# 64 unused bytes ahead of the split weights of a two-layer hybrid decoder trunk

## The chip, the cores and the metric

The kernel runs on one core of one Trainium2 chip. The metric is the device time of one execution in microseconds (us); lower is better. The timed runs of the kernel before agree within 0.3 us, so a difference of 0.2%, some 2.4 us, can be told from none.

## The reference, cut to what matters

512 tokens of width 1024 go through two layers. Each layer is a token mixer (mLSTM in the first, differential attention in the second) beside a cross-attention into 256 memory tokens, an output projection and a SwiGLU feed-forward of hidden width 2816:

```python
for i in range(DEPTH):                       # two layers
    h = rmsnorm(x, norm1[i])
    mix, xq = mlstm_mixer(h, ...) if i % 2 == 0 else diff_attention(h, positions, ...)
    xo = memory_cross_attention(xq, mem, ...)
    x = x + jnp.concatenate([mix, xo], axis=-1) @ w_out[i]
    h = rmsnorm(x, norm2[i])
    gu = h @ w_gate_up[i]
    x = x + (jax.nn.silu(gu[..., :FFN_HIDDEN]) * gu[..., FFN_HIDDEN:]) @ w_down[i]
```

All is float32. Nearly all arithmetic is in the products of activations with weights.

## The kernel before

**Split operands.** A float32 operand is kept as the sum of two rounded ones, a high and a low part, both in the type F32R. A product of two such operands is three matmuls that accumulate in the same PSUM bank: weights high by tokens high, weights high by tokens low, weights low by tokens high. For each matmul TensorE first loads its 128 x 128 stationary operand (the weights) and then streams the moving operand (the tokens) past it. The profile lists the two as PEld LDWEIGHTS and PE MATMUL, and writes the moving operand first: `PS<-Hh,w_hi` streams Hh past w_hi.

**Three kinds of product use the split weights.**

- *Dense products*, by `tile` (L1948), with 512 moving columns. The tokens are Hh and Hl (the normalised input, 560 sets of three) or Ah and Al (mixer output or hidden units, 480 sets of three). They make the projections, the output projections, the first gate and up tiles of each feed-forward, and all down tiles.
- *Memory products*, by `m_tile` (L1983), through the same `tile`, with 256 moving columns out of Ah and Al: 64 sets of three.
- *Block products*, by `pair` (L2262, matmul at L2284), with 256 moving columns. For 16 of 22 hidden chunks of each layer, the gate and up tiles are made together in a Strassen-like scheme: seven block products with tokens tc_hi and tc_lo and weights w_hi and w_lo, each of four steps k of three matmuls. That is 2 layers x 16 x 7 x 4 = 896 sets of three.

The matmuls of the first two kinds are recorded under the helper's line L1946, with the attention's matmuls, which use no split weights; the block products have L2284 to themselves. Beside them, in the first 17 us, `wg` (the eight gate columns, padded to 128) is multiplied with Hh and Hl, 16 matmuls.

**Where operands lie.** SBUF tensors are taken one after the other in the order of the code (L276 to L283 and on), each rounded up to 32 bytes a partition, so a tensor's byte address in its partition follows from the sizes ahead of it. Of the operands of the F32R products:

| tensor | address before | modulo 256 | step from one operand to the next |
|---|---|---|---|
| Hh, Hl, Ah, Al | 17,536; 33,920; 50,304; 66,688 | 128 | 2048 B dense, 1024 B memory |
| w_raw (weights as loaded) | 83,072 | 128 | 512 B |
| w_hi, w_lo | 99,456; 113,792 | 128 | 512 B |
| tc_hi, tc_lo | 169,152; 197,824 | 192 | 1024 B |
| wg | 218,112 | 0 | 512 B |

All steps are multiples of 256 bytes, so every operand of a tensor has the tensor's place modulo 256. Dense and memory products have weights at 128 and tokens at 128; block products have weights at 128 and tokens at 192; the gate columns have weights at 0 and tokens at 128.

**Order of the work.** Each engine's program is written out by hand. SyncE loads weight tiles from HBM into the four slots of w_raw. GpSimd (POOL) splits them for dense tiles (L778 writes w_hi, L783 writes w_lo) and forms sums and differences of weight tiles for the block products (L736 to L743) and part of their low parts (L748); ScalarE and VectorE round and split the rest and move PSUM to SBUF. Semaphores carry the order.

```python
w_raw = sb("w_raw", [P, RAW, 8, P])
wq_hi = sb("w_hi", [P, 28, P], F32R)
wq_lo = sb("w_lo", [P, 28, P], F32R)
```

Of the kernel before, what the change touches and what calls it, by code (L numbers as in the profile page):

```python
# [32 lines left out]
P = 128  # L33
# [230 lines left out]
def hybrid_trunk(nc, x_t, mem_t, positions, wt, wg_cols, a_gate_b, b_lambda, prm_cols, con, out):  # L264
    ctx = ExitStack()
    with ctx:
        def sb(name, shape, dt=F32, scope=ctx):
            return scope.enter_context(nc.sbuf_tensor(name, shape, dt))
# [10 lines left out]
        Ah = sb("Ah", [P, 8, SEQ], F32R)  # L279
        Al = sb("Al", [P, 8, SEQ], F32R)  # L280
        w_raw = sb("w_raw", [P, RAW, 8, P])
        wq_hi = sb("w_hi", [P, 28, P], F32R)
        wq_lo = sb("w_lo", [P, 28, P], F32R)  # L283
        w_hi = wq_hi[:, 0:8 * SPLIT].rearrange("p (s k) m -> p s k m", k=8)
# [2331 lines left out]
```

## Time and profile before

| | us |
|---|---|
| median of 3 runs (1202.67 to 1202.94) | 1202.91 |
| the profiled execution, as timed | 1204.02 |
| its span, first to last instruction | 1202.2 |
| TensorE matmul (PE) busy | 1196.8 |
| GpSimd (POOL) busy | 857.4 |
| VectorE (DVE) busy | 755.9 |
| ScalarE (ACT) busy | 502.4 |

A matmul's own duration in these tables, say 389 ns, runs from its start to its last result, and matmuls overlap in the array. What one costs in a stream is the distance between the starts of neighbours; it is read from the timeline, or from a piece of the chain of waits divided by its count.

### The profile page before, as it was taken

The page shows a single profiled execution, that of the slowest core. Times are in us where ns is not written, and L with a number is a line of the kernel's source. Part 1 is how long each engine was busy: PE and PEld are TensorE (multiplying, and loading weights), DVE is VectorE, ACT ScalarE, POOL GpSimd, SP SyncE. Part 2 cuts the span into 40 slices and gives each one's busy share as a digit, 9 for nine tenths or more (in the row PEclk, how much of TensorE's full clock was granted, in tenths as well). Part 3 has the DMA queues.
Part 4 walks back from the last instruction along what each step waited for, and adds up shares of the span by engine and source line. Part 5 has one row for each costly group of instructions (what it writes and reads, how often), then busy time and mean ns, then how long its engine had stood idle before and what let it go on. Part 6 is the DMA issues. An engine that isn't in the chain of part 4 may idle for free.

```text
span 1202.2 us, 18736 instructions
## 1 busy us (share of the span) xinstructions
PE 1196.8 (100%) x6998; PEld 1032.9 (86%) x6998; DVE 755.9 (63%) x1099; ACT 502.4 (42%) x1012; POOL 857.4 (71%) x873
## 2 busy tenths in 40 slices
PE   9999999999999999999999999999999999999998
PEld 7888887788889998899888777778888899889997
DVE  7954434645737991599335888874674599348931
ACT  7522456733203551355231666644431255125510
POOL 7998433566878996699676444445688799669965
PEclk9999999999999999999999999999999999999999
DMA  7234211132223333233433222232232333322332
GB/s 282 92 123 157 71 36 53 53 106 79 92 83 106 106 106 123 88 106 106 126 103 97 80 71 71 64 80 69 71 100 79 118 106 107 105 89 98 115 105 85
DMA packets 35097, 117.43 MB, mean 98 GB/s; under 512 B 4417, under 2 KB 4930, under 8 KB 34886
## 3 DMA queue, kind: packets, MB, share of 16 engines
q1 hardware_dynamic: 33416, 112.83, 29.2%
q10 hardware_dynamic: 1598, 3.51, 1.2%
q8 instruction: 51, 0.84, 0.3%
q14 instruction: 32, 0.26, 0.1%
HBM read 111.07 MB, written 2.11 MB: 94 GB/s over the span
## 4 chain that ended last, share of the span: by engine, by line
PE 97%; DVE 1%; ACT 1%; issue 0%; ACTq 0%; POOL 0%; POOLq 0%
PE PS L1946 69%; PE PS L2284 26%; PE PS L2385 1%; DVE Al L1564 0%; PE PS L2194 0%; PE PS L2413 0%; PE PS L2354 0%; DVE nmB L1850 0%; PE PS L2019 0%; PE PS L2346 0%; PE PS L2338 0%; DVE PB L1862 0%; ACT tmp L1010 0%; ACT tmp L1018 0%; DVE PB L1861 0%
## 5 line engine op out<-in xcount | busy, mean ns | idle before, releaser
L783 POOL TENSOR_TENSOR w_lo<-w_raw,w_hi 128x256 fp32r<-128x256 f32 (+1 forms) x516 | 394.7, 796 | 11.0
L778 POOL TENSOR_SCALAR w_hi<-w_raw 128x1024 fp32r<-128x1024 f32 (+2 forms) x132 | 142.1, 1076 | 283.4 <-PE PS L1946 275.0
L2284 PE MATMUL PS<-tc_hi,w_hi 128*128 128x256 f32 x896 | 250.9, 280 | 0.0
L2284 PE MATMUL PS<-tc_hi,w_lo 128*128 128x256 f32 x896 | 250.0, 279 | 0.0
L2284 PE MATMUL PS<-tc_lo,w_hi 128*128 128x256 f32 x896 | 250.0, 279 | 0.0
L1946 PE MATMUL PS<-Hh,w_hi 128*128 128x512 f32 x560 | 229.3, 410 | 0.0
L1946 PE MATMUL PS<-Hl,w_hi 128*128 128x512 f32 x560 | 219.1, 391 | 0.0
L1946 PE MATMUL PS<-Hh,w_lo 128*128 128x512 f32 x560 | 219.0, 391 | 0.0
L1946 PE MATMUL PS<-Ah,w_hi 128*128 128x512 f32 (+1 forms) x544 | 208.0, 382 | 0.1
L1946 PE MATMUL PS<-Ah,w_lo 128*128 128x512 f32 (+1 forms) x544 | 205.0, 377 | 0.0
L1946 PE MATMUL PS<-Al,w_hi 128*128 128x512 f32 (+1 forms) x544 | 204.9, 377 | 0.0
L2284 PEld LDWEIGHTS PS<-tc_hi,w_lo 128*128 128x128 f32 x896 | 168.5, 188 | 0.0
L2284 PEld LDWEIGHTS PS<-tc_hi,w_hi 128*128 128x128 f32 x896 | 168.2, 188 | 0.2
L2284 PEld LDWEIGHTS PS<-tc_lo,w_hi 128*128 128x128 f32 x896 | 167.6, 187 | 0.2
L1619 DVE TENSOR_TENSOR xT<-xT,PS 128x512 f32<-128x512 f32 x64 | 43.9, 687 | 159.4 <-PE PS L1946 159.4
L1946 PEld LDWEIGHTS PS<-Hh,w_hi 128*128 128x128 f32 x560 | 105.6, 189 | 27.6 <-issue 7.8
L1946 PEld LDWEIGHTS PS<-Hh,w_lo 128*128 128x128 f32 x560 | 105.4, 188 | 22.8
L1946 PEld LDWEIGHTS PS<-Hl,w_hi 128*128 128x128 f32 x560 | 105.7, 189 | 20.2 <-issue 1.0
L748 POOL TENSOR_TENSOR w_lo<-tmp,w_hi 128x512 fp32r<-128x512 f32 x64 | 107.7, 1700 | 17.9 <-ACT w_hi L1099 17.9
L1946 PEld LDWEIGHTS PS<-Ah,w_hi 128*128 128x128 f32 x544 | 102.3, 188 | 20.7 <-issue 1.5
L1946 PEld LDWEIGHTS PS<-Ah,w_lo 128*128 128x128 f32 x544 | 102.3, 188 | 19.0
L1946 PEld LDWEIGHTS PS<-Al,w_hi 128*128 128x128 f32 x544 | 102.4, 188 | 18.6 <-issue 0.5
(300 smaller groups left out, 1805.5 us busy)
## 6 DMA issues: line engine op xcount, KB each, us to landing
w_raw<-in_wt_dram SPq DMA_DIRECT2D x181, 512.0 KB, 3.6
w_raw<-in_wt_dram SPq DMA_DIRECT2D x16, 384.0 KB, 3.0
w_raw<-in_wt_dram SPq DMA_DIRECT2D x8, 448.0 KB, 3.3
QKR<-QKP ACTq DMA_DIRECT2D x24, 128.0 KB, 4.8
xT<-in_x_t_dram SPq DMA_DIRECT2D x8, 256.0 KB, 4.8
out_dram<-xT SPq DMA_DIRECT2D x8, 256.0 KB, 2.0
mT<-in_mem_t_dram SPq DMA_DIRECT2D x1, 1024.0 KB, 9.5
cn<-in_constants_dram SPq DMA_DIRECT2D x1, 594.5 KB, 6.9
```

The source lines that it names most:

```text
L748: nc.gpsimd.tensor_tensor(wq_lo[:, b:b + 4], pair_source(n, q), wq_hi[:, b:b + 4].bitcast(F32), ALU.subtract).then_inc(s_low_p, 1)
L778: nc.gpsimd.tensor_scalar(w_hi[:, sl, 0:nk], w_raw[:, raw, 0:nk], 0.0, 1.0, ALU.add, ALU.mult).then_inc(w_round, 1)
L783: lo = nc.gpsimd.tensor_tensor(w_lo[:, sl, w], w_raw[:, raw, w], w_hi[:, sl, w].bitcast(F32), ALU.subtract)
L1619: nc.vector.tensor_tensor(xT[:, k], xT[:, k], PS[:, bank], ALU.add).then_inc(dense_free, 1)
L1946: return nc.tensor.matmul(out_, a, b, start=start, stop=stop)
L2284: last = nc.tensor.matmul(out_, w[:, b + k], a[:, q, k], start=q < 4 and k == 0 and j == 0, stop=k == 3 and j == 2, skip_group_check=q > 3)
L2385: last = nc.tensor.transpose(PS[:, 2 + u % 2, k * P:(k + 1) * P], PB[:, 0, W_OFF[u] + k * P:W_OFF[u] + (k + 1) * P], ident)
```

## The change

One tensor of 16 float32 a partition, 64 bytes, is put between w_raw and w_hi. Nothing reads or writes it.

```diff
@@ -279,6 +279,7 @@
         Ah = sb("Ah", [P, 8, SEQ], F32R)
         Al = sb("Al", [P, 8, SEQ], F32R)
         w_raw = sb("w_raw", [P, RAW, 8, P])
+        sb("shift_w", [P, 16])
         wq_hi = sb("w_hi", [P, 28, P], F32R)
         wq_lo = sb("w_lo", [P, 28, P], F32R)
         w_hi = wq_hi[:, 0:8 * SPLIT].rearrange("p (s k) m -> p s k m", k=8)
```

xT, Hh, Hl, Ah, Al and w_raw stay where they are; every tensor behind moves up by 64 bytes. The built programs have the same 10,478 instructions in the same order on every engine, with the same waits; only addresses differ, and line numbers by one.

| product | weights, tokens modulo 256 before | after | tokens minus weights before | after |
|---|---|---|---|---|
| dense, memory | 128, 128 | 192, 128 | 0 | -64 |
| block | 128, 192 | 192, 0 | +64 | +64 |
| gate columns | 0, 128 | 64, 128 | 128 | +64 |

## Rows read from the trace of the kernel before

**Rows 1.** The page's part 1: engine, busy us, share of the span, instructions.
```profile
PE 1196.8 (100%) x6998; PEld 1032.9 (86%) x6998; DVE 755.9 (63%) x1099; ACT 502.4 (42%) x1012; POOL 857.4 (71%) x873
```

**Rows 2.** Waits of TensorE, whole span: waited for, us in total, times, longest.
```profile
PE PS L1946 <- POOL hpi L700: 1.0, 1, 1.0
PE PS L1946 <- ACT PB L1216: 0.5, 1, 0.5
PE PS L2385 <- ACT ATB L1225: 0.4, 1, 0.4
```

**Rows 3.** The chain of waits: start us, us, what, instructions in the piece.
```profile
377.26 79.15 PE PS L2284 x672
499.97 79.15 PE PS L2284 x672
...
953.63 79.15 PE PS L2284 x672
1076.34 79.15 PE PS L2284 x672
```

**Rows 4.** Groups of TensorE matmuls by form: shapes, count | busy us, mean ns | idle.
```profile
L2284 PE MATMUL PS<-tc_hi,w_hi 128*128 128x256 f32 x896 | 250.9, 280 | 0.0
...
L1946 PE MATMUL PS<-Hh,w_hi 128*128 128x512 f32 x560 | 229.3, 410 | 0.0
...
L1946 PE MATMUL PS<-Ah,w_hi 128*128 128x512 f32 x480 | 188.7, 393 | 0.1
...
L1946 PE MATMUL PS<-Ah,w_hi 128*128 128x256 f32 x64 | 19.3, 302 | 0.0
```

**Rows 5.** Timeline, memory products (start us, us, instruction); ten like them left out.
```profile
52.54 0.28 PE L1946 MATMUL PS<-Ah,w_lo 128*128 128x256 f32 x1
52.66 0.28 PE L1946 MATMUL PS<-Ah,w_hi 128*128 128x256 f32 x1
...
53.98 0.28 PE L1946 MATMUL PS<-Ah,w_lo 128*128 128x256 f32 x1
```

**Rows 6.** Timeline, dense products of a down stage; 47 left out.
```profile
469.66 0.39 PE L1946 MATMUL PS<-Ah,w_lo 128*128 128x512 f32 x1
...
480.54 0.39 PE L1946 MATMUL PS<-Ah,w_lo 128*128 128x512 f32 x1
```

**Rows 7.** Timeline, last block product and first dense ones behind it.
```profile
1032.50 0.28 PE L2284 MATMUL PS<-tc_hi,w_lo 128*128 128x256 f32 x1
1032.62 0.40 PE L1946 MATMUL PS<-Ah,w_hi 128*128 128x512 f32 x1
1032.86 0.39 PE L1946 MATMUL PS<-Al,w_hi 128*128 128x512 f32 x1
...
1034.24 0.39 PE L1946 MATMUL PS<-Al,w_hi 128*128 128x512 f32 x1
1034.47 0.39 PE L1946 MATMUL PS<-Ah,w_lo 128*128 128x512 f32 x1
```

**Rows 8.** Timeline of the start: dense products and gate columns in turn; nine left out.
```profile
11.94 0.39 PE L1946 MATMUL PS<-Hh,wg 128*128 128x512 f32 x1
...
14.27 0.39 PE L1946 MATMUL PS<-Hh,wg 128*128 128x512 f32 x1
```

**Rows 9.** Stretches: length, busy (x) of PE, PEld, DVE, ACT, POOL, PEclk, DMA, GB/s.
```profile
14.00:16.00 2.00, 2.00 (x10) 1.60 (x9) 1.90 (x4) 0.96 (x2) 2.00 (x3) 1.00 1.06 446
...
19.00:20.00 1.00, 1.00 (x6) 0.84 (x5) 0.65 (x1) 0.00 (x0) 1.00 (x2) 1.00 1.02 406
```

**Rows 10.** The same view: first block stage, a down stage, the second layer's attention.
```profile
377.00:456.00 79.00, 79.00 (x672) 78.96 (x671) 67.91 (x92) 41.47 (x82) 74.15 (x51) 1.00 0.32 113
456.00:500.00 44.00, 44.00 (x198) 36.49 (x197) 13.19 (x16) 7.20 (x11) 26.30 (x30) 1.00 0.27 87
...
650.00:830.00 180.00, 178.91 (x1043) 140.24 (x1042) 138.76 (x255) 105.73 (x279) 84.37 (x100) 0.99 0.26 71
```

**Rows 11.** Timeline, attention scores: tokens and stationary operand both at 192, two half-height matmuls each.
```profile
663.17 0.28 PE L1946 MATMUL PS<-QR_LO,QT_HI 64*128 64x256 f32 x2
663.29 0.28 PE L1946 MATMUL PS<-QT_HI,QR_LO 64*128 64x256 f32 x2
```

**Rows 12.** Timeline, the first products after the gate columns; three left out.
```profile
18.45 0.39 PE L1946 MATMUL PS<-Hh,w_lo 128*128 128x512 f32 x1
...
19.36 0.39 PE L1946 MATMUL PS<-Hh,w_hi 128*128 128x512 f32 x1
```

**Rows 13.** The page's part 5, the split of the low parts on GpSimd.
```profile
L783 POOL TENSOR_TENSOR w_lo<-w_raw,w_hi 128x256 fp32r<-128x256 f32 (+1 forms) x516 | 394.7, 796 | 11.0
```

## The prediction, on record before the result

> **What bounds the kernel now.** I read the page's busy shares first: TensorE's matmuls are busy 1196.8 of 1202.2 us, the next engine 857.4 [rows 1]. Then TensorE's waits: 1.9 us in all, in three waits [rows 2]. The chain of waits says the same from the other end, with whole stages in single pieces of TensorE, 672 block products in 79.15 us four times over [rows 3]. So the time is the number of matmuls times what each costs in the stream. No other engine matters until TensorE becomes quicker than it. The granted clock is 1.00 in all stretches used here, the 2.4 GHz level [rows 9, 10].
>
> **What one matmul costs, and what of it is not columns.** Durations in the groups [rows 4] overlap and don't serve; distances of starts do.
>
> - Memory products, 256 columns: twelve steps from 52.54 to 53.98 us, 1.44 / 12 = 120.0 ns each [rows 5].
> - Dense products, 512 columns: 48 steps from 469.66 to 480.54 us, 10.88 / 48 = 226.7 ns each [rows 6].
> - Their difference, 106.7 ns for 256 columns, is 0.417 ns a column, one period of 2.4 GHz. So 256 columns are 106.7 ns, 512 are 213.3 ns, and either kind pays the same 13.3 ns on top.
> - Block products, 256 columns as well: 79.15 us / 672 = 117.8 ns [rows 3], only 11.1 ns on top.
>
> Memory and block products have the same shape, the same kinds of operand and a weight load each. What differs is where the tokens lie: 128 modulo 256 for the first, 192 for the second, with weights at 128 in both. Over a set of three the block products save 3 x 2.22 = 6.7 ns, which is the time of 16 columns, and 16 columns of tokens are 64 bytes. That such a round figure comes out is my reason to take the surplus for something that hangs on addresses in steps of 64 bytes, and not for a property of the stage.
>
> **Place or distance?** The surplus could hang on where the tokens lie, where the weights lie, or how far they are apart. The attention scores have tokens and stationary operand both at 192, and one pair follows the other after 0.12 us at 256 columns [rows 11]: 120 ns, as where both are at 128. These are half-height matmuls, two side by side, so it is a weak witness, but it speaks for distance: 0 gives 13.3, +64 gives 11.1. The third distance is seen at the start. There two of five products use the gate columns, with weights at 0 and tokens at 128, distance 128, and ten steps take 14.27 - 11.94 = 2.33 us, 233.0 ns each, 19.7 ns on top [rows 8]. DMA isn't the reason: its engines are full then and are still full at 19 to 20 us [rows 9], when the gate columns are over and four steps from 18.45 to 19.36 us take 0.91 us, 227 ns each [rows 12]. So distances of 0, +64 and 128 are seen, and the dense products go to the one that is not seen, -64.
>
> **The change, part by part.**
>
> 1. *Dense and memory products, distance 0 to -64.* They are 3120 and 192, 3312 in all (each count in the table of groups is one of three) [rows 4]. The nearest rows are 11.1 ns (distance +64) and 19.7 ns (a mix with 128) against 13.3 now. If -64 is as good as +64, that is -2.22 x 3312 = -7.4 us. If it is as bad as the mix with 128, it is (233.0 - 226.7) x 3312 = +20.9 us. I take -7.4 us: one step of 64 bytes off alignment is what the better row has, to one side, and the other side is equally one step off.
> 2. *Block products, +64 kept, but tokens from 192 to 0 and weights from 128 to 192.* By distance this costs nothing. Bounds: losing the whole surplus, 2688 x 11.1 = -29.8 us; going to the memory products' 120.0 ns, +5.9 us. I take 0, by the row in which both operands at 192 cost what both at 128 cost [rows 11].
> 3. *Gate columns, distance 128 to +64.* Sixteen matmuls among 24 dense ones; if all forty come from 233.0 to 224.4 ns, -0.3 us. Left out.
> 4. *Products whose two operands both move* (attention scores, transposes, sums over partitions) keep their distance: 0.
> 5. *Splits on GpSimd, rounding on ScalarE and VectorE.* They write w_hi and w_lo at 192 instead of 128 and read w_raw where it was. I have no row of one operation at both places, so from below and above a few per cent either way. The cover is TensorE: in a block stage GpSimd is busy 74.15 of 79.0 us, in a down stage 26.3 of 44 [rows 10]. A split slower by up to 6% stays hidden; beyond that each block stage would end with GpSimd. 0.
> 6. *DMAs.* They fill w_raw, which stays; the few between moved tensors stand behind waits that cost 1.9 us in all [rows 2]. 0.
> 7. *Transients.* After a stage ends, the dense products don't take 226.7 ns at once: behind a block stage seven steps from 1032.62 to 1034.24 us take 231.4 each [rows 7]. In the second layer's attention, dense products stand between short matmuls and are mostly in that state (1043 matmuls in 180 us) [rows 10]. What the shift makes of them isn't seen; I price them like the steady ones.
>
> Sum: -7.4 us against the execution that was profiled (span 1202.2, timed at 1204.02). That one is 1.1 us above the median, and a saving per matmul carries over unchanged: 1202.9 - 7.4 = 1195.5 us.
>
> One rule speaks against any effect. TensorE has two SBUF read ports, one for the moving operand and one for weights, and loading the next weights takes nothing from the running matmul (the Trainium skill, TensorE: Matmul & The Clock Gate, step-by-step: what each phase is for). By it the sum would be 0 and the time 1202.9 us. The trace doesn't agree so far as it goes: two streams of one shape cost 120.0 and 117.8 ns.
>
> **The rivals.**
>
> *Nothing moves, 1202.9 us.* The 2.2 ns would then be the block stage's own, from the tensors' distance in whole kilobytes or the way banks are taken in turn, or -64 would cost what 0 costs. For it: one pair of kinds is thin evidence. Against it: the gate columns differ from dense products in address and in bank alone, and they cost more [rows 8, 12].
>
> *The wrong side: dense products slower, 1210 to 1224 us.* With tokens 64 bytes behind the weights instead of ahead, the two reads could meet where now they pass. Seen around the circle of 256 bytes, the surplus is 13.3 at 0, 11.1 at +64 and high at 128; -64 lies between 0 and the high one, with no low neighbour but 0. One step of 16 columns more on each of 1104 sets is +7.4 us, 1210.3. Staying at the 233.0 ns of the start is +20.9, 1223.8; if the attention stages, already near that, lose nothing, about half is left, 1213. It decides from the point at which the dense distance goes above 227 ns; GpSimd can't offset it. This is nearly as likely as my forecast.
>
> *Place counts in the block products.* Tokens at 0 begin a stretch of 256 bytes. If half the surplus goes, 2688 x 5.5 = -14.9 us, but GpSimd's 74.15 of 79.0 us caps the gain at 4.9 us a stage, 19 us in all [rows 10]: with dense unchanged about 1188. If they go to 120.0 ns, 1208.8. For: nothing; against: rows 11.
>
> **How the numbers follow.** Forecast (dense and memory gain one step, block unchanged) 0.33, with its own range 1193 to 1199; no change 0.18; dense slower 0.32, a third of that near 1210 and the rest up to 1224; block products faster, alone or with the dense, 0.11; block products slower 0.06. Faster by over 0.2% is 0.33 + 0.11 = 0.44, slower 0.32 + 0.06 = 0.38, within 0.2% (all that a measurement can tell from no change) 0.18. Cases of both signs hold most of the chance. The range is 1189 to 1221: it leaves out the far end of the slow case, about 0.1, and large gains in the block products or in the dense beyond one step, about 0.08.
>
> **What would show it.** In the changed kernel's timeline a steady stretch of dense products should show 224.4 ns from start to start instead of 226.7, memory products 117.8 instead of 120.0, and the four block pieces of the chain 79.15 us again. TensorE's waits should stay near 2 us. Dense at 226.7 means no effect; at 229 or 233 the wrong side. Block pieces away from 79.15 us mean that the place counts, and then the sum above is built on the wrong variable. GpSimd's mean for a low part well away from its 796 ns [rows 13] would say that its writes depend on the place too.

## The result, and the profile after

| | before | changed |
|---|---|---|
| median, us | 1202.84 (1202.67 to 1202.94, 4 runs) | 1218.01 (1217.85 to 1219.42, 4 runs) |
| span of the profiled execution, us | 1202.2 | 1216.1 |

The changed kernel takes 1.0127 times as long, 95% interval 1.0113 to 1.0141: 15.2 us slower. The forecast was 1195.5 us, faster.

The page's busy shares and TensorE's waits of the changed kernel, as in [rows 1, 2]:

```profile
PE 1210.7 (100%) x6998; PEld 1030.9 (85%) x6998; DVE 754.8 (62%) x1099; ACT 502.1 (41%) x1012; POOL 857.2 (70%) x873
...
PE PS L1947 <- POOL hpi L701: 1.0, 1, 1.0
PE PS L1947 <- ACT PB L1217: 0.5, 1, 0.5
PE PS L2386 <- ACT ATB L1226: 0.4, 1, 0.4
```

TensorE is 13.9 us busier, every other engine is as busy as before to 2 us, and the waits are the same three to a tenth. Nothing became late; the matmuls themselves take longer. The chain of waits (start us, us, what, instructions) says which. The rows of after:

```profile
383.29 79.14 PE PS L2285 x672
462.44 44.80 PE PS L1947 x192
507.23 79.15 PE PS L2285 x672
...
1044.24 44.80 PE PS L1947 x192
1089.04 79.14 PE PS L2285 x672
```

and the down stage between the same block stages before, which is not among the rows above:

```profile
456.41 43.56 PE PS L1946 x192
```

Three of the four block stages are what they were in [rows 3], 79.15 us; the third is not one piece here and comes further down. The down stage, 192 dense products, went from 43.56 to 44.80 us, 1.24 us. The timeline gives the price of one product (start us, us, instruction; 44 rows left out), in the changed kernel:

```profile
475.34 0.40 PE L1947 MATMUL PS<-Ah,w_lo 128*128 128x512 f32 x1
...
485.84 0.39 PE L1947 MATMUL PS<-Ah,w_lo 128*128 128x512 f32 x1
```

45 steps in 10.50 us are 233.3 ns each, where [rows 6] had 226.7: 20.0 ns over the columns' 213.3 instead of 13.3. The 256-column memory products went the other way. Twelve steps of the changed kernel:

```profile
87.08 0.28 PE L1947 MATMUL PS<-Ah,w_hi 128*128 128x256 f32 x1
...
88.44 0.28 PE L1947 MATMUL PS<-Ah,w_hi 128*128 128x256 f32 x1
```

1.36 / 12 = 113.3 ns, where [rows 5] had 120.0. That is this stretch; in others of the changed kernel many memory products still take 118 ns.

**Which profile to compare with.** The medians are 15.2 us apart, the two profiled spans only 13.9. The profiled execution of the kernel before lost time to something else. Its windows (length, busy and count of PE, PEclk, DMA, GB/s):

```profile
780.00:792.00 12.00, 11.58 (x72) 1.00 0.51 121
...
793.00:796.00 3.00, 3.00 (x12) 0.50 0.41 108
```

For some 3.4 us the granted clock is 0.50, the 1.2 GHz level, and before it TensorE had been busy in 80.00 of the 80 us from 700 to 780. This is the 0.99 that [rows 10] show for 650 to 830 us. The changed kernel's profile has no such stretch, so a comparison by stage needs another one. Run e13 below has all addresses modulo 256 as before, a median of 1203.1 us, a granted clock of 1.00 in 780 to 800 us and a span of 1200.8 us. Its chain, and then that of the changed kernel at the third block stage:

```profile
377.56 79.15 PE PS L2285 x672
...
579.41 75.96 PE PS L1947 x349
...
952.24 79.15 PE PS L2285 x672
```

```profile
965.43 13.62 PE PS L2285 x120
```

By stage, from starts of the pieces: the first 377.6 us (1248 dense and all 192 memory products) grew by 5.7 us, the three down stages between and behind block stages by 1.2 each, the stretch from the second to the third block stage (1296 dense products) from 372.8 to 379.1 us, by 6.2, and the third block stage shrank by 0.3. The sum is 15.3 us, which is the spans' difference, 1216.1 - 1200.8.

3120 dense products at +6.7 ns would be 20.8 us. Averages over all starts in the two traces say what is missing. Outside the down stages, 2307 dense products are followed at once by another dense one; this step went from 227.6 to 233.3 ns, which is 13.2 us, and the down stages add 3.7. The other 237 are followed by a product of another kind or by a longer step, and those hardly changed. The step of 227.6 instead of 226.7 ns comes from the attention stages: in the second layer's, 650 to 830 us, 319 such steps averaged 229.8 ns, while in the stretches on either side it was 226.8. The memory products gave 0.8 us back.

GpSimd's split of low parts took what it took in [rows 13]:

```profile
L784 POOL TENSOR_TENSOR w_lo<-w_raw,w_hi 128x256 fp32r<-128x256 f32 (+1 forms) x516 | 394.9, 796 | 11.0
```

### The profile page after: what moved, and what is told of

It reads as the page before. It is cut to its first block, busy times and chain, and to the rows that moved or that the text cites. A ratio compares the mean times of both kernels' runs of the same rounds, so it can differ in the third digit from the quotient of the medians.

```text
span 1216.1 us, 18736 instructions
## 1 busy us (share of the span) xinstructions
PE 1210.7 (100%) x6998; PEld 1030.9 (85%) x6998; DVE 754.8 (62%) x1099; ACT 502.1 (41%) x1012; POOL 857.2 (70%) x873
## 4 chain that ended last, share of the span: by engine, by line
PE 98%; DVE 1%; DMA 0%; issue 0%; ACT 0%; POOL 0%; ACTq 0%; SPq 0%; DVEq 0%; POOLq 0%
PE PS L1947 70%; PE PS L2285 26%; PE PS L2386 1%; PE PS L2195 0%; PE PS L2414 0%; DMA w_raw<-in_wt_dram 0%; DVE nmB L1851 0%; PE PS L2355 0%; PE PS L2347 0%; PE PS L2020 0%; PE PS L2339 0%; DVE PB L1863 0%; PE PS L2158 0%; PE PS L2155 0%; DVE PB L1862 0%
## 5 line engine op out<-in xcount | busy, mean ns | idle before, releaser
L1947 PE MATMUL PS<-Al,w_hi 128*128 128x512 f32 (+1 forms) x544 | 207.5, 381 | 0.0
L1947 PE MATMUL PS<-Ah,w_lo 128*128 128x512 f32 (+1 forms) x544 | 207.5, 381 | 0.0
```

The costliest lines, as they stand in the source:

```text
L1947: return nc.tensor.matmul(out_, a, b, start=start, stop=stop)
```

## The experiments

All differ from the kernel before by unused bytes alone, with the same instructions in the same order. The diffs that show a `-` line start from the changed kernel, the others from the kernel before. `[P, n]` is n float32, 4n bytes. "Distance" is tokens minus weights modulo 256. The columns "192 dense" and "672 block" are pieces of the chain of waits, a down stage and a block stage.

| run | weights | dense distance | block distance | 192 dense, us | 672 block, us | median, us | ratio, 95% |
|---|---|---|---|---|---|---|---|
| before | 128 | 0 | +64 | 43.56 | 79.15 | 1202.9 | |
| changed | 192 | -64 | +64 | 44.80 | 79.14 | 1218.0 | 1.0127 (1.0113 to 1.0141) |
| e1_w192 | 64 | +64 | +64 | 43.96 | 77.86 to 78.85 | 1207.2 | 1.0037 (1.0023 to 1.0051) |
| e2_w128 | 0 | 128 | +64 | 44.62 | 79.15 | 1216.4 | 1.0113 (1.0092 to 1.0133) |
| e3_w_only | 192 | -64 | 0 | 44.80 | 80.63 | 1224.1 | 1.0176 (1.0159 to 1.0193) |
| e4_all64 | 192 | 0 | +64 | 43.56 | 79.15 | 1202.7 | 0.9997 (0.9987 to 1.0006) |
| e5_tc64 | 128 | 0 | -64 | 43.52 | 79.15 | 1202.5 | 0.9997 (0.9987 to 1.0006) |
| e6_tc0 | 128 | 0 | 128 | 43.56 | 80.64 | 1209.0 | 1.0051 (1.0031 to 1.0071) |
| e7_dense_m32 | 160 | -32 | +32 | 44.80 | 78.40 | 1215.8 | 1.0107 (1.0087 to 1.0128) |
| e9_tc160 | 128 | 0 | +32 | 43.55 | 78.40 | 1199.9 | 0.9975 (0.9966 to 0.9985) |
| e10_tc96 | 128 | 0 | -32 | 43.57 | 79.52 | 1204.9 | 1.0016 (1.0007 to 1.0026) |
| e11_tc224 | 128 | 0 | +96 | 43.56 | 80.64 | 1208.6 | 1.0044 (1.0028 to 1.0060) |
| e12_dense_p32 | 96 | +32 | +96 | 44.79 | 80.64 | 1224.9 | 1.0181 (1.0161 to 1.0202) |
| e13_pad256 | 128 | 0 | +64 | 43.56 | 79.15 | 1203.1 | 1.0002 (0.9991 to 1.0013) |

### Place or distance

Two theories went in. Theory A: the distance alone counts. Theory C: the place of the weights counts.

```diff
+        sb("shift_x", [P, 16])
         xT = sb("xT", [P, KD, SEQ])
```

> The 64 unused bytes lie ahead of xT, so that Hh, Hl, Ah, Al, w_raw and all others move with the weights: every distance is that of the kernel before (dense 0, block +64), every place is 64 bytes on. Theory A (distance alone): 226.7 and 117.8 ns, 1202.9 us. Theory C (the place of the weights at 192): dense at 233.3 ns as in the changed kernel, 1218 us.

Measured: 1202.67 us, ratio 0.9997. The weights begin at 192 and the block tokens at 0, the very places that the change gives them, and nothing is lost. Its chain:

```profile
377.32 79.15 PE PS L2285 x672
456.47 43.56 PE PS L1947 x192
```

Theory C falls: weights at 192 cost nothing as long as the tokens are at 192 too.

```diff
         w_raw = sb("w_raw", [P, RAW, 8, P])
+        sb("shift_w", [P, 16])
         wq_hi = sb("w_hi", [P, 28, P], F32R)
         wq_lo = sb("w_lo", [P, 28, P], F32R)
...
+        sb("shift_c", [P, 48])
         cn = sb("cn", [P, N_CON])
```

> 64 bytes ahead of the split weights and 192 more behind them, so that the weights alone are moved modulo 256 (weights 192, block tokens 192 as in the kernel before, everything else at its old place modulo 256). Dense distance -64, block distance 0. Theory A: dense as in the changed kernel, 233.3 ns (+20.8 us if all of them, +15 us as measured there), and the block products go from 117.8 to the 120.0 ns that memory products had at distance 0, +5.9 us: some 1224 us. If the place of the tokens counts for the block products and not the distance, they stay at 117.8 ns: 1218 us.

Measured: 1224.1 us, the 1224 that theory A gave. Its chain:

```profile
383.32 80.63 PE PS L2286 x672
463.95 44.81 PE PS L1948 x192
```

80.63 / 672 = 120.0 ns a block product, which is what memory products cost at distance 0 in [rows 5]. So the 2.2 ns between the two kinds in the kernel before was their distance and nothing else. The dense ones are as in the changed kernel.

```diff
-        sb("shift_w", [P, 16])
+        sb("shift_w", [P, 64])
```

> 256 unused bytes ahead of the split weights: all addresses modulo 256 are those of the kernel before, distances modulo 512 are not (the dense one goes from 0 to 256). If 256 bytes are the whole circle: 1202.9 us, dense 226.7 and block 117.8 ns, to a tenth. If the circle is wider: dense off 226.7 ns, as it is at every other distance tried, and over 1205 us.

Measured: 1203.11 us, 43.56 and 79.15 us in the chain. Moving by 256 bytes changes nothing. Moving by 128 does (e2, below), so among powers of two the circle is 256.

### The other distances of dense products

```diff
-        sb("shift_w", [P, 16])
+        sb("shift_w", [P, 48])
```

> 192 unused bytes ahead of the split weights instead of 64: weights at 64 modulo 256, block tokens at 128. Tokens minus weights is +64 for dense, memory and block products. Theory A (what counts is the distance, and each 64 bytes of it are worth 16 columns, 6.7 ns a dense product: -64 gave 233.3, 0 gives 226.7): dense products come at 220.0 ns, 3120 x -6.7 = -20.8 us, so some 1182 us. Theory B (any distance but 0 disturbs the dense products): dense at about 233 ns, 1218 us. Theory C (the weights' own place counts, and 128 is the good one): dense slower than 226.7 ns too, by an amount it can't name.

Measured: 1207.23 us. Theories A and B miss; theory C named no amount, and e4 has ruled it out. Dense products don't gain at +64; they lose 0.40 us in 192, 2.1 ns each, a third of what -64 costs. Theory A as a ramp of 6.7 ns per 64 bytes is dead; that distance counts is not.

The block stages of this run are worth a look, since their distance is as before and still they changed. From the chain:

```profile
395.54 9.76 PE PS L2285 x84
405.30 9.76 PE PS L2285 x84
415.09 42.64 PE PS L2285 x360
```

and ten steps in the timeline of that stretch:

```profile
399.81 0.28 PE L2285 MATMUL PS<-tc_lo,w_hi 128*128 128x256 f32 x1
...
400.94 0.28 PE L2285 MATMUL PS<-tc_hi,w_lo 128*128 128x256 f32 x1
```

1.13 us / 10 = 113 ns, against 117.8 before at the same distance. Late in the same run, in its last block stage, it is the old rhythm again (17 rows left out):

```profile
1139.81 0.28 PE L2285 MATMUL PS<-tc_lo,w_hi 128*128 128x256 f32 x1
...
1141.93 0.28 PE L2285 MATMUL PS<-tc_lo,w_hi 128*128 128x256 f32 x1
```

2.12 / 18 = 117.8 ns. A stream of 256 columns at +64 has two rhythms; what decides between them is not shown. At 113.3 ns a pair of tiles, 84 products, would take 9.52 us, but only the first and the last of a quick stage do. In the second block stage of this run the chain breaks once a pair:

```profile
501.69 16.32 PE PS L2285 x144
...
518.12 9.76 PE PS L2285 x84
...
527.89 9.76 PE PS L2285 x84
...
567.07 12.48 PE PS L2285 x108
579.55 0.46 PE PS L1947 x2
```

From 518.12 to 567.07 us five pairs start 9.77 to 9.80 us apart. The break of some 0.2 us is not in the table of waits, because a matmul's own 0.28 us cover it; it shows in the starts and in the gaps of the chain. At 527.9 us:

```profile
527.32 0.42 DVE L1727 TENSOR_TENSOR tmp<-PS,tmp 128x256 f32<-128x256 f32 x1
...
527.60 0.28 PE L2285 MATMUL PS<-tc_hi,w_lo 128*128 128x256 f32 x1
...
527.89 0.35 PE L2285 MATMUL PS<-tc_hi,w_hi 128*128 128x256 f32 x1
```

TensorE goes on 0.15 us after VectorE has joined a finished block product. Over one such pair the windows show GpSimd as the fullest of the other engines:

```profile
547.50:557.30 9.80, 9.76 (x85) 9.60 (x85) 8.96 (x13) 5.58 (x11) 9.55 (x7) 1.00 0.29 105
```

GpSimd is busy in 9.55 of 9.80 us, VectorE in 8.96. So in the quick rhythm the other engines set the pace of a pair, VectorE last and very likely GpSimd behind it; which of the two one would have to relieve was not tried. The whole stage took 579.55 - 501.69 = 77.86 us, the shortest of any run, against 79.15.

```diff
-        sb("shift_w", [P, 16])
+        sb("shift_w", [P, 32])
```

> 128 unused bytes ahead of the split weights: weights at 0, block tokens at 64; dense distance 128, block distance +64. Theory A: dense at 240.0 ns (one more step past -64) or, if the circle closes here, 213.3 ns: 1203 + 41.6 = 1244 us or 1161 us. Theory B: about 1218 us. Block products unchanged at 117.8 ns by both.

Measured: 1216.43 us. Dense products at 128 take 44.62 us in 192, nearly what -64 takes; neither number of theory A came, and theory B's 1218 was near for this run while e1 denies it.

```diff
+        sb("shift_w", [P, 8])
         wq_hi = sb("w_hi", [P, 28, P], F32R)
...
+        sb("shift_c", [P, 56])
         cn = sb("cn", [P, N_CON])
```

> 32 bytes ahead of the split weights and 224 behind: weights at 160, block tokens at 192. Dense distance -32, block distance +32. If the cost goes evenly with distance, dense products come halfway between 226.7 and 233.3, at 230.0 ns: +10 us; block products between 120.0 and 117.8 ns, +3 us: 1216 us. If steps of 64 bytes count alone, dense stays at 226.7 or is at 233.3 ns at once.

Measured: 1215.8 us. Its chain:

```profile
383.78 78.40 PE PS L2286 x672
462.18 44.80 PE PS L1948 x192
```

32 bytes off already cost dense products all of the 1.24 us that 64 bytes cost; there is no halfway, and a step of 64 bytes isn't the unit. The total came as expected by two wrong halves: the block products at +32 are quicker than at +64, not slower, and that pays for part.

The other side, 224 bytes ahead of the weights and 32 behind (`shift_w` of 56 and `shift_c` of 8):

> 224 bytes ahead of the split weights and 32 behind: weights at 96, block tokens at 192. Dense and memory distance +32, block distance +96. Dense at +64 came at 229.2 ns and at 0 at 226.7, so at +32 between them, 228 ns, if the cost goes evenly: 1203 + 3120 x 1.3 = 1207 us with block unchanged. If only distance 0 is spared: 233 ns, +20 us, 1218 us and more, as at -32.

Measured: 1224.89 us; 44.79 us for 192 dense. At +32 they lose as much as at -32, and more than at +64. Distance 0 is a narrow good place for 512 columns. The 80.64 us of the block stage (distance +96) add 4 x 1.49 = 6.0 us, most of what this run is slower than the changed kernel.

### The distance of block products alone

Padding behind w_lo, ahead of cn, leaves dense products at 0 and moves the block tokens. Of the five runs only the length of that one tensor differs.

> 128 unused bytes behind the split weights and none ahead: weights at 128 as in the kernel before, block tokens at 64. Dense and memory distance 0 as before, block distance -64. Theory D (distance counts, and short 256-column streams like what long ones don't: the memory products came at 113.3 ns at -64): block products mostly at 113.3 instead of 117.8 ns, 2688 x -4.4 = -12 us, dense at 226.7: some 1191 us, unless GpSimd, busy 74 us of each block stage, ends them at more than 76 us. Rival (block products at -64 lose as dense ones did): slower than 1203 us, at 120 ns +6 us.

Measured: 1202.54 us. At -64 block products cost 79.15 us a stage, as at +64. Theory D's quick rhythm did not come, nor did the rival's loss. Memory products show that rhythm at -64 in a stretch of the changed kernel, so the distance alone doesn't bring it.

> 64 unused bytes behind the split weights alone: weights at 128, block tokens at 0, so the tokens stand where the change puts them and the weights where they were. Dense distance 0, block distance 128. Theory D: dense at 226.7 ns; block products at 128 are not yet seen, memory products there had a mix with mean 120 ns: 1203 to 1209 us. Rival (tokens at 0 are good in themselves): faster than 1203 us.

Measured: 1209.01 us, 80.64 us a stage. Tokens that begin a stretch of 256 bytes are not good in themselves.

> 32 unused bytes behind the split weights: dense and memory distance 0, block distance +96 (weights 128, block tokens 224). Between +64 (117.8 ns) and 128 (120.0 ns): 118.9 ns and 1206 us if the cost is even in between, 117 ns and 1201 us if odd multiples of 32 are a class of their own.

Measured: 1208.62 us, 80.64 us, 120.0 ns: the same as at 128, and above both expectations.

> 160 unused bytes behind the split weights: dense and memory distance 0, block distance -32 (weights 128, block tokens 96). If the block cost is even about 0 as +64 and -64 were (117.8 ns both): 116.7 ns, 1200 us. If -32 is the costly side as for dense products: 120 ns or more, 1209 us or more.

Measured: 1204.87 us, 79.52 us, 118.3 ns each: neither expectation. +32 and -32 don't cost the same.

```diff
         wq_lo = sb("w_lo", [P, 28, P], F32R)
+        sb("shift_c", [P, 56])
         cn = sb("cn", [P, N_CON])
```

> 224 unused bytes behind the split weights, none ahead: dense and memory distance 0, block distance +32 (weights 128, block tokens 160). With -32 for the dense products the block products stood at +32 and came at 116.7 instead of 117.8 ns. If the block cost hangs on its own distance: 116.7 ns again, 2688 x -1.1 = -3 us, dense at 226.7 ns: 1200 us, faster than the kernel before. If it hung on the state the dense products left behind: 117.8 ns, 1203 us.

Measured: 1199.9 us, ratio 0.9975 (0.9966 to 0.9985), the one version that is faster than the kernel before beyond its interval. Its chain:

```profile
377.84 78.40 PE PS L2285 x672
456.24 43.55 PE PS L1947 x192
499.79 78.40 PE PS L2285 x672
```

Four block stages at 78.40 instead of 79.15 us are 3.0 us, all of the gain. A pair takes 78.40 / 8 = 9.80 us here, with no breaks. In e1, quicker matmuls brought the steady pairs no lower than 9.77 to 9.80, so little is left to gain from the rhythm: 0.5 us a stage against e1's best.

### Within a set of three

```diff
         wq_hi = sb("w_hi", [P, 28, P], F32R)
+        sb("shift_lo", [P, 16])
         wq_lo = sb("w_lo", [P, 28, P], F32R)
+        sb("shift_c", [P, 48])
```

> 64 bytes between w_hi and w_lo and 192 behind w_lo: only the low weights move, to 192; dense distance is 0 with w_hi and -64 with w_lo. Theory E (what lengthens a product is the load of the next one's weights while it streams): of each set of three dense products only the second, which streams tokens low while w_lo is loaded, changes; surplus +6.7 ns on one of three, some +7 us in all, 1210 us. Rival (a product's own weights and tokens): only the third changes, with the same sum. The distances of starts by place in the set tell the two apart.

Measured: 1212.44 us (1.0080, 1.0059 to 1.0100). From its timeline:

```profile
475.02 0.40 PE L1948 MATMUL PS<-Ah,w_lo 128*128 128x512 f32 x1
475.26 0.39 PE L1948 MATMUL PS<-Ah,w_hi 128*128 128x512 f32 x1
475.49 0.39 PE L1948 MATMUL PS<-Al,w_hi 128*128 128x512 f32 x1
475.72 0.40 PE L1948 MATMUL PS<-Ah,w_lo 128*128 128x512 f32 x1
```

The step behind the third product (own weights w_lo, the next one's w_hi) is the longest, 0.24 against 0.23 and 0.23, and a matmul's own duration, which follows that step, is 0.40 there alone. That is where a product's own weights would have it. But over the down stage a set takes 44.40 us / 64 = 694 ns against 43.56 / 64 = 681 undisturbed: 13 ns more and not 7. Averaged over the starts from 468 to 498 us, the step behind the third product is 236 ns, 9 more than undisturbed, and the other two are 228 and 229: they are longer as well.

```diff
+        sb("shift_w", [P, 16])
         wq_hi = sb("w_hi", [P, 28, P], F32R)
+        sb("shift_lo", [P, 48])
         wq_lo = sb("w_lo", [P, 28, P], F32R)
```

> Only w_hi is moved, to 192; w_lo and all others stand where they were modulo 256. Of each dense set the first and second product have own weights at distance -64, the third 0. If a product's own weights and tokens count: the first two steps of a set are the long ones, the third 226.7 ns. If the load of the next product's weights beside the stream counts: the steps with w_hi loaded beside them, the third and the first, are long. Either way about two thirds of the changed kernel's loss, 1213 us; the earlier run with w_lo alone moved lost 9.5 us, so a sum that isn't additive would show here as well.

Measured: 1216.74 us (1.0117, 1.0088 to 1.0147).

```profile
475.03 0.40 PE L1948 MATMUL PS<-Ah,w_lo 128*128 128x512 f32 x1
475.26 0.40 PE L1948 MATMUL PS<-Ah,w_hi 128*128 128x512 f32 x1
475.50 0.39 PE L1948 MATMUL PS<-Al,w_hi 128*128 128x512 f32 x1
475.73 0.40 PE L1948 MATMUL PS<-Ah,w_lo 128*128 128x512 f32 x1
```

Here the rows with the longer duration, 0.40, are the third and the first, those beside which w_hi is loaded: the other theory. The averages are 235 and 236 ns behind these two and 229 behind the second. The down stage is 44.78 us, 700 ns a set, all of what moving both costs (44.80). But the last down stage of this same run, with the same addresses, has another rhythm:

```profile
1167.14 44.39 PE PS L1948 x192
```

That is 694 ns a set. Two rhythms at one distance are not a matter of 256 columns alone, and the step that is longest here may be one of several that these addresses allow. Nor does an uneven set by itself say which product is off: in e1, where all three are at +64, the averages are 226, 229 and 232 ns. So one run speaks for a product's own weights and the other for the next one's, and neither explains both.

```diff
         Hh = sb("Hh", [P, KD, SEQ], F32R)
+        sb("shift_a", [P, 48])
         Hl = sb("Hl", [P, KD, SEQ], F32R)
+        sb("shift_b", [P, 16])
         Ah = sb("Ah", [P, 8, SEQ], F32R)
+        sb("shift_c", [P, 48])
         Al = sb("Al", [P, 8, SEQ], F32R)
+        sb("shift_d", [P, 16])
         w_raw = sb("w_raw", [P, RAW, 8, P])
```

> Only the low parts of the tokens, Hl and Al, are moved, to 64 modulo 256; weights, Hh and Ah stand where they were. The second product of each dense set has distance -64, the others 0. If each product pays for its own distance alone: only the second step is long, 233.3 ns, +6.7 x 1040 = +7 us, 1210 us. If a set settles into one rhythm that all three share: more than that, and spread over the steps, as in the run with w_lo alone moved.

Measured: 1207.35 us (1.0040, 1.0021 to 1.0060).

```profile
475.05 0.39 PE L1950 MATMUL PS<-Al,w_hi 128*128 128x512 f32 x1
475.28 0.39 PE L1950 MATMUL PS<-Ah,w_lo 128*128 128x512 f32 x1
475.51 0.39 PE L1950 MATMUL PS<-Ah,w_hi 128*128 128x512 f32 x1
475.74 0.39 PE L1950 MATMUL PS<-Al,w_hi 128*128 128x512 f32 x1
```

One product of three is off, and all three steps are 0.23, on average 228 to 229 ns: here the set shares one rhythm, as it did not in e8. The down stage is 43.97 us, 687 ns a set, 6 ns more than undisturbed, once.

Over the runs, a dense set takes 43.56, 43.97, 44.40 or 44.80 us / 64 = 681, 687, 694 or 700 ns. The steps between are 6 to 7 ns, which is 16 columns of 0.417 ns. e1, with all three at +64, has 43.96 us, 687 ns; the run at distance 128, at 697 ns, lies between two of the values.

## Why the prediction was wrong

**What bounds the kernel** was right: TensorE's stream, with the same 1.9 us of waits before and after, and at most 2.1 in any other run. The exception is block stages in the quick rhythm (parts of e1 and of the changed kernel's third stage), where the other engines set the pace. The prediction read a clock of 1.00 in all its stretches; [rows 10] have 0.99 in one of them, and the stretch at half clock behind it is why its profile lay 1.1 us above the median. The forecast didn't hang on it.

**Distance, not place** was right, and so was the reading of 13.3 against 11.1 ns as a matter of addresses: e4, with places moved and distances kept, gave 1202.7 us, and e3 turned 117.8 ns into 120.0 by distance alone. This stood on one pair of kinds and one weak witness, and it might have gone the other way.

**The step that failed** is the first of the change's parts, the -7.4 us for distance -64: "the other side is equally one step off". It put dense products at 224.4 ns, and the steady ones took 233.3. It had two main faults, and a smaller one beside them: 64 bytes aren't the unit of the effect, since 32 already cost dense products all of the 1.24 us (e7).

- *The sign of a distance matters, and a neighbour says little.* At 256 columns +64 and -64 do cost the same (79.15 us both), but +32 and -32 don't (78.40 and 79.52), and at 512 columns +64 costs 43.96 and -64 44.80 us.
- *A row at 256 columns doesn't price 512 columns.* This is the one that turned the sign. The better value at +64 was read from block products of 256 columns and given to dense products of 512. The runs show that distance 0 is the best for 512 columns, of six tried, while at 256 columns it has the worst value of seven tried, 120.0 ns, with +96 and 128. No row of the kernel before had 512 columns at +64; e1 shows that even that cost 0.40 us per 192 and not a gain. The memory products did what the forecast hoped and more, 120.0 to 113.3 ns in the stretch shown, but they are 192 of 3312.

**The sizes.** -7.4 us was forecast for dense and memory products; +16.9 came for the dense and -0.8 for the memory products, with 0.8 off for all else, 15.3 us in all. The bound worked out beside it, +20.9 us from the 233.0 ns of the start [rows 8], was within 0.3 ns of what one steady dense product came to cost, 233.3 ns. What it overstated was how many products stood at 226.7 before. That rival gave 1210 to 1224 us and held the result. It got 0.32 against 0.33 for the forecast, though one row of the trace with 512 columns off distance 0 stood for it [rows 8] and none with 512 columns stood for the forecast.

**Block products** kept 79.15 us in three of four stages, as predicted. In the third stage, a part ran in the quick rhythm that e1 showed, which gave 0.3 us. The cap of 4.9 us a stage, read from GpSimd's 74.15 of 79.0 us, was too wide: the shortest stage of any run gained 1.3 us. A share of busy time says when an engine is full at the latest, not when it begins to hold others up.

**Splits** were taken as 0, and GpSimd's mean for a low part is 796 ns in both kernels. **Gate columns, products with both operands moved, DMAs**: taken as 0 too. They were not measured apart; all that isn't dense, memory or block products changed by about 0.5 us in sum.

**Transients**: "I price them like the steady ones" was a mis-sized term. All 3120 at the steady price would be 20.8 us, and 16.9 came. "Mostly in that state" was too much for the second layer's attention: in e13, 157 of its 319 steps from one dense product to the next were at 230 ns or more, and the mean was 229.8. They still lost 3.5 ns each; about 4 us is what all transients and stage ends kept back, and not the 10 that the rival at 1213 assumed.

**The rule on read ports** that the prediction set against itself says that loading the next weights takes nothing from the running matmul (the Trainium skill, TensorE: Matmul & The Clock Gate, step-by-step: what each phase is for). Read as "addresses cost no time" it would have made all runs equal, and they span 1199.9 to 1224.9 us with the same instructions. So that reading fails here. Whether it is the load that takes the time, no run shows; what meets what inside stays open.

**Left open**: whether a product is held up by its own operands' distance or by that of the next one's weights (e8 says the one, e14 the other, e15 that a set shares one rhythm); why one distance can have two rhythms (113 and 117.8 ns at 256 columns in e1, 694 and 700 ns a set at 512 in e14); and distances between multiples of 32 bytes, which weren't tried.

## What to carry to other kernels

In this kernel, bound by TensorE's F32R stream, the place of a few unused bytes moved the time by 2% (1199.9 to 1224.9 us). Where another kernel is bound so, it is worth a try: work out the operands' addresses modulo 256, and take tokens minus weights as the variable. Fix it separately for each length of the moving operand, and give those with most time to lose the choice first; here that is 0 for 512 columns and +32 for 256. Compare profiles only after a look at the granted clock of both: 3.4 us at half clock hid a tenth of this change. A price for a shape is read from a row of the same shape, or it isn't a price but a guess; where a trace has only the other shape, a range to both sides is the honest answer, and the one row with the right shape outweighs all of the wrong one.

## What the runs showed of the hardware

- The distance between an F32R matmul's moving and stationary operand in a partition, modulo 256 bytes, changes its cost: at 512 columns from 226.9 to 233.3 ns (43.56 and 44.80 us / 192), at 256 columns from 116.7 to 120.0 ns (78.40 and 80.64 us / 672), and in the quick rhythm 113. Moving both by 64 bytes changes nothing (1202.7 against 1202.9 us), and moving the weights by 256 nothing either (1203.1).
- At 256 columns one distance, +64, was seen at 113 and at 117.8 ns a product, in stages of one and the same run (e1).
- In a set of three accumulating products with different distances the cost isn't confined to those that are off: with one of three off the set took 687 ns in e15 and 694 in e8 instead of 681, and each of the three steps was longer.
- The block stages are 1.3 us a stage away from being bound by the other engines: with matmuls at 113 ns, pairs of tiles still start 9.77 to 9.80 us apart, and the shortest stage took 77.86 us.
- One stretch of 3.4 us at a granted clock of 0.50 in the profile of the kernel before goes with a span of 1202.2 us, where e13 without it had 1200.8; e4's profile has such a stretch too, and 1202.2 us.
